# MLP weights of a fused decoder layer: a plain piece as one k tile by 1024 columns instead of two k tiles by 512

## The chip, the core and the metric

The kernel runs as one program on one core of a Trainium2 chip. A core has a matrix engine (TensorE, "PE" in the rows; its weight loads are "PEld"), a vector engine (VectorE, "DVE"), a scalar engine (ScalarE, "ACT"), a general engine (GpSimd, "POOL") and a sync engine (SyncE, "SP"), which here issues every DMA. The engines run their own instruction streams in order and wait for each other by semaphores. The metric is the device time of one execution in microseconds (us), as a median over runs.

## What is computed

One decoder layer in fp32 for 256 tokens and a width of 2048: three token mixers, their gated sum, an output projection, and then the MLP that the change is about.

```python
merged = g[:, :, 0] * o_conv + g[:, :, 1] * o_fox + g[:, :, 2] * o_mem
x = x + merged @ w_out
h2 = _rms(x, norm2_g)
x = x + jnp.square(jax.nn.relu(h2 @ w_up)) @ w_down   # w_up 2048 x 8192, w_down 8192 x 2048
```

## The kernel before

**How products are made.** Tokens are in two tiles of 128 (`TOK = 2`). Activations are the stationary operand (128 by 128), weights the moving one (128 by 512). Each fp32 product is three passes on split operands: low activations by high weights, high by high, high by low. So a weight tile `raw` that DMA brings is split by ScalarE into `whi` (line 591, `split`) and by VectorE into `wlo = raw - whi` (line 1009), and TensorE then uses both. There are `RING = 4` slots of 128 by 1024 for `raw`, `whi` and `wlo`. The semaphore `lo_ready` counts pieces split; `piece_used` counts pieces that TensorE is through with.

**How the MLP is cut.** D_FF is taken in four quarters (`QUARTERS`) of 2048. A quarter has four blocks (`blk` 0 to 3) of 1024 output columns: 0 and 1 multiply by `w_up` (stationary operand `lhs_b`), 2 and 3 by `w_down` (stationary operand `lhs_a`, the squared ReLU of the first two). A block has eight groups of two k tiles (`at` 0 to 7, in the order `K_ORDER`), and a group is 256 rows by 1024 columns of weights. Of the eight groups six are *plain* and two are *fast* (`FAST_AT`): a fast group loads all its 1 MB at once into `raw_f`, and makes seven products in place of eight from sums of weight quarters, formed by VectorE (`t_sums`, lines 1311 to 1316), split by ScalarE (line 794) and VectorE (line 1320); the remaining quarters are split by lines 802 and 1326. Fast products run at line 1801. `raw_f` is a single buffer: SyncE reloads it (line 520) when line 1326 of the fast group before is done. "Fast (3, 5)" below is the one at place 5 of block 3.

A plain group is two *pieces*, n and n + 1, each a 512 KB DMA (line 524) and twelve matmuls (line 1780). Before the change piece n is the *left* half of the block's columns (banks 0 and 1, `side` 0) for both k tiles, and piece n + 1 the *right* half (banks 2 and 3, `side` 1). PSUM banks 0 to 3 hold the block's sums by side and token tile.

**Between blocks.** The sums are copied out of banks 0 and 1, then 2 and 3, by ScalarE (`c_copy`, line 892, 128 by 1024 each, to the buffers named `stage` and `junk`), which counts `c_out`; TensorE may start the next block's left sums after the first copy and its right sums after the second. Blocks 0 to 2 end with a fast group, in which the four banks are finished 15 and 12 matmuls before the group's end. Block 3 ends with a plain group at place 7 (its fast groups are at 2 and 5), and there the first copy waits for the left piece and the second for the right piece. ScalarE's order at the start of a quarter is written out by hand:

```python
upper(0, 0)          # splits of group 0, left and right
if q:
    c_copy(0, 0)
left(0, 1)           # split of the next group's first piece
if q:
    c_copy(0, 1)
right(0, 1)
```

Three places are at such a *quarter boundary*, where a block 3 is followed by a block 0. After the fourth block 3 VectorE adds the result straight from the banks (line 1544 for the left half, two instructions of line 1548 for the right), and SyncE stores the left half in one DMA of 512 KB (line 550) and the right in two of 256 KB (line 555).

Of the kernel before, what the change touches and what calls it, by code (L numbers as in the profile page):

```python
# [25 lines left out]
P = 128  # L26
D = 2048
TOK = 2
KT = D // P
# [7 lines left out]
PK = 2  # L37
# [147 lines left out]
def is_fast(n):  # L185
    if n < first(B_FF):
        return False
    _, blk, at, _ = ff_place(n)
    return at in FAST_AT[blk]
# [73 lines left out]
def build(nc, t, out):  # L263
    ctx = ExitStack()
    with ctx:
# [10 lines left out]
        def sem(name):  # L276
            return ctx.enter_context(nc.semaphore(name))
# [118 lines left out]
        t_made, t_hi_ready, t_lo_ready = sem("t_made"), sem("t_hi_ready"), sem("t_lo_ready")  # L396
        fast_landed, fast_made = sem("fast_landed"), sem("fast_made")
        a_copied, s_made = sem("a_copied"), sem("s_made")
        s_hi_ready, s_lo_ready = sem("s_hi_ready"), sem("s_lo_ready")
# [46 lines left out]
        def _(sp):  # L446
# [66 lines left out]
            def load_ff(n, src, base=0):  # L513

                if is_fast(n):
                    if freed_by(n) < 0:
                        sp.wait_ge(merged_ready, NBD)
                    else:
                        sp.wait_ge(lo_ready, base + (freed_by(n) + 1))
                    sp.dma_start(raw_f[:].rearrange("p (k s) n -> p k (s n)", k=PK), src).then_inc(fast_landed, 16)  # L520
                    return
                sp.wait_ge(lo_ready, base + (freed_by(n) + 1))
                slot = plain(n) % RING
                sp.dma_start(raw[slot], src).then_inc(landed[slot], 16)

            for n in load_order(0):
                _, blk, at, side = ff_place(n)
                k = slice(PK * K_ORDER[blk][at], PK * (K_ORDER[blk][at] + 1))
                c = WIDE * (blk % UPS) + COLS * side
                if is_fast(n) and side:  # L530
                    continue
                width = WIDE if is_fast(n) else COLS
                load_ff(n, w_up[:, k, c:c + width] if blk < UPS else w_down[0, :, k, c:c + width])

            with sp.Fori(0, QUARTERS - 1) as i:
                for n in load_order(1):
                    _, blk, at, side = ff_place(n)
                    k = slice(PK * K_ORDER[blk][at], PK * (K_ORDER[blk][at] + 1))
                    c = WIDE * (blk % UPS) + COLS * side
                    if is_fast(n) and side:  # L540
                        continue
                    width = WIDE if is_fast(n) else COLS
                    if blk < UPS:
                        src = w_up[:, k, bass.ds(i * D + (D + c), width)]
                    else:
                        src = w_down_rows[:, bass.ds(i * KT + (KT + k.start), PK), c:c + width]
                    load_ff(n, src, base=i * FF_PIECES)
# [35 lines left out]
        def _(act):  # L583
# [258 lines left out]
            def quarter(q, i):  # L842
# [39 lines left out]
                def c_copy(blk, side):  # L882

                    pq, pblk, number = block_of_sums(blk)
                    if GROUPS - 1 in FAST_AT[pblk]:
                        act.wait_ge(fast_made, by_f * 5 + (5 * last_fast(pq, pblk) + 1 + side))
                    else:
                        act.wait_ge(piece_used, by_n + (ff_piece(q, blk) - 1 + side))
                    if number:
# [113 lines left out]
        def _(dve):  # L1003
# [538 lines left out]
            dve.wait_ge(x_in, UPS * QUARTERS)  # L1542
            dve.wait_ge(piece_used, ff_piece(QUARTERS) - 1)
            dve.tensor_tensor(x_half(UPS - 1, 0), bank_all[:, 0:2, :], comb[:, 0:2, :],
# [8 lines left out]
        def _(pe):  # L1553
# [217 lines left out]

            def half_group(n, side, k, at, lhs, stops):


                pe.wait_ge(lo_ready, n + 1)
                hi, lo = whi[n % RING], wlo[n % RING]
                for kk in range(PK):
                    for tok in range(TOK):
                        for i, (part, w) in enumerate(((1, hi), (0, hi), (0, lo))):
                            last = pe.matmul(bank[2 * side + tok],  # L1780
                                             lhs[:, part, PK * k + kk, P * tok:P * (tok + 1)], w[:, kk, :],
                                             start=(at + kk == 0 and i == 0),
                                             stop=(tok in stops and kk == PK - 1 and i == 2))
                last.then_inc(piece_used, 1)
# [50 lines left out]
            for n in range(ff_piece(0), ff_piece(QUARTERS)):  # L1835
# [19 lines left out]
                if at == 0 and number == 0:  # L1855
                    pe.wait_ge(dve_emptied, emptied(B_WO + 2))
                elif at == 0:
                    pe.wait_ge(c_out, 2 * (number - 1) + side + 1)
                if number == 0:
# [4 lines left out]
                plain_last = GROUPS - 1 not in FAST_AT[blk]  # L1864
                stops = ()
                if at == GROUPS - 1:
                    stops = (0, 1)
                elif at == GROUPS - 2 and not plain_last and side == 0:
                    stops = (0,)
                half_group(n, side, k, at, lhs, stops)  # L1870

# [36 lines left out]
```

## Time and profile before

| what | us |
|---|---|
| median of 3 runs | 1637.64 (1636.01 to 1638.37) |
| the profiled execution, its own time | 1635.64 |
| its span, first to last instruction | 1633.9 |
| TensorE busy in it | 1624.5 |
| VectorE busy | 1101.9 |
| ScalarE busy | 851.6 |
| granted TensorE clock | 1.000 of full over the span |

The span leaves out 1.74 us of the profiled execution's time. Spans and waits below are from that one execution. A row of the timeline gives start, duration, engine, line, operation, output and inputs, how many instructions were merged in it, and in brackets how long the engine had been idle and whose end released it. Matmuls overlap in the pipeline, so the distance between two starts, not the duration, says how fast they go.

### The profile page before, as it was taken

To read this page: it belongs to the slowest core of one execution; us is meant where nothing else is said; L and a number is where in the kernel's file an instruction comes from. 1 tells how busy PE (TensorE), PEld (TensorE's weight loads), DVE (VectorE), ACT (ScalarE), POOL (GpSimd) and SP (SyncE) were. 2 spreads that over 40 slices of the span, in tenths; PEclk is the share of its full clock that TensorE was granted. 3 is DMA by queue.
4 is the path that set the end of the run, shared out by engine and by line. 5 is a ranking of instruction groups with operands and counts; after the bars stand their busy time and mean duration, and the time that the engine had idled before them with its cause. 6 is when DMAs were issued, how large, how long until landed. Compare 5 with 4: busy or idle time off the path is not lost.

```text
span 1633.9 us, 20167 instructions
## 1 busy us (share of the span) xinstructions
PE 1624.5 (99%) x7404; PEld 1345.7 (82%) x7404; DVE 1101.9 (67%) x1199; ACT 851.6 (52%) x1002; POOL 4.8 (0%) x13
## 2 busy tenths in 40 slices
PE   8999999999999999999999999999999999999998
PEld 7888888888888888888888888888888888888887
DVE  5856666545465444456665678887878788887777
ACT  5844445443454444444344566655665466555663
POOL 0000000000000000000000000000000000000000
PEclk9999999999999999999999999999999999999999
DMA  9866565566666666765666665566656565665554
GB/s 323 286 176 185 166 181 151 158 171 175 170 180 185 194 190 191 199 192 182 197 188 184 209 189 177 192 201 196 204 188 198 191 197 184 203 206 188 191 188 153
DMA packets 151486, 313.70 MB, mean 192 GB/s; under 512 B 9072, under 2 KB 9456, under 8 KB 150896
## 3 DMA queue, kind: packets, MB, share of 16 engines
q1 hardware_dynamic: 151408, 312.62, 62.1%
q8 instruction: 54, 0.88, 0.2%
q14 instruction: 24, 0.20, 0.0%
HBM read 310.49 MB, written 2.10 MB: 191 GB/s over the span
## 4 chain that ended last, share of the span: by engine, by line
PE 93%; DVE 3%; DMA 2%; issue 1%; ACT 1%; SPq 0%; DVEq 0%; ACTq 0%
PE bank L1567 53%; PE bank L1780 28%; PE bank L1801 8%; PE bank L1584 2%; DMA raw_f<-in_w_down 1%; PE bank L1597 1%; DVE wlo L1009 1%; DMA raw<-in_w_mem_kv 1%; DVE wlo L1326 1%; ACT whi L591 0%; DVE t_raw L1311 0%; DVE t_lo L1320 0%; PE bank L1692 0%; PE bank L1622 0%; PE bank L1653 0%
## 5 line engine op out<-in xcount | busy, mean ns | idle before, releaser
L1009 DVE TENSOR_TENSOR wlo<-raw,whi 128x1024 fp32r<-128x1024 f32 x510 | 619.2, 1223 | 440.6 <-ACT whi L591 437.6
L591 ACT ACTIVATE whi<-raw 128x1024 fp32r<-128x1024 f32 x510 | 537.5, 1058 | 585.5 <-PE bank L1567 393.7
L1567 PE MATMUL bank<-whi,lhs_a 128*128 128x512 f32 x1920 | 598.2, 393 | 0.0
L1567 PEld LDWEIGHTS bank<-whi,lhs_a 128*128 128x128 f32 x1920 | 357.2, 188 | 71.7
L1567 PE MATMUL bank<-wlo,lhs_a 128*128 128x512 f32 x960 | 374.7, 390 | 0.0
L1780 PE MATMUL bank<-whi,lhs_b 128*128 128x512 f32 x768 | 237.6, 391 | 0.0
L1780 PE MATMUL bank<-whi,lhs_a 128*128 128x512 f32 x768 | 237.5, 391 | 0.0
L1567 PEld LDWEIGHTS bank<-wlo,lhs_a 128*128 128x128 f32 x960 | 180.3, 188 | 38.1
L1780 PEld LDWEIGHTS bank<-whi,lhs_a 128*128 128x128 f32 x768 | 143.6, 188 | 29.4
L1780 PEld LDWEIGHTS bank<-whi,lhs_b 128*128 128x128 f32 x768 | 143.5, 188 | 29.3
L1567 PE MATMUL bank<-whi,lhs_b 128*128 128x512 f32 x512 | 158.3, 391 | 3.2 <-DVE wlo L1032 2.5
L1780 PE MATMUL bank<-wlo,lhs_b 128*128 128x512 f32 x384 | 149.7, 390 | 0.0
L1780 PE MATMUL bank<-wlo,lhs_a 128*128 128x512 f32 x384 | 149.7, 390 | 0.0
L1567 PEld LDWEIGHTS bank<-whi,lhs_b 128*128 128x128 f32 x512 | 95.7, 188 | 24.1 <-issue 4.5
L1567 PE MATMUL bank<-wlo,lhs_b 128*128 128x512 f32 x256 | 99.8, 390 | 0.0
L1780 PEld LDWEIGHTS bank<-wlo,lhs_a 128*128 128x128 f32 x384 | 72.1, 188 | 15.0
L1780 PEld LDWEIGHTS bank<-wlo,lhs_b 128*128 128x128 f32 x384 | 72.1, 188 | 15.0
L1320 DVE TENSOR_TENSOR t_lo<-t_raw,t_hi 128x2048 fp32r<-128x2048 f32 x32 | 73.1, 2285 | 4.5 <-ACT t_hi L794 4.5
L802 ACT ACTIVATE whi<-raw_f 128x1536 fp32r<-128x1536 f32 x32 | 47.6, 1487 | 54.2 <-PE bank L1780 54.2
L1326 DVE TENSOR_TENSOR wlo<-raw_f,whi 128x1536 fp32r<-128x1536 f32 x32 | 56.1, 1754 | 26.0 <-ACT whi L802 26.0
L794 ACT ACTIVATE t_hi<-t_raw 128x1024 fp32r<-128x1024 f32 x64 | 64.5, 1047 | 13.6 <-DVE t_raw L1311 11.7
L1567 PEld LDWEIGHTS bank<-wlo,lhs_b 128*128 128x128 f32 x256 | 48.0, 188 | 10.1
(200 smaller groups left out, 1253.4 us busy)
## 6 DMA issues: line engine op xcount, KB each, us to landing
raw<-in_w_in SPq DMA_DIRECT2D x208, 512.0 KB, 3.8
raw<-in_w_up SPq DMA_DIRECT2D x96, 512.0 KB, 4.1
raw<-in_w_down SPq DMA_DIRECT2D x96, 512.0 KB, 4.6
raw<-in_w_out SPq DMA_DIRECT2D x32, 512.0 KB, 4.5
raw_f<-in_w_up SPq DMA_DIRECT2D x16, 1024.0 KB, 5.0
raw_f<-in_w_down SPq DMA_DIRECT2D x16, 1024.0 KB, 5.2
raw<-in_w_mem_kv SPq DMA_DIRECT2D x30, 512.0 KB, 6.9
raw<-in_w_conv_out SPq DMA_DIRECT2D x16, 512.0 KB, 4.5
```

Of the source, the lines that this page charges most:

```text
L591: act.activation(whi[n % RING], raw[slot], ACT.Copy).then_inc(hi_ready, 1)
L794: act.activation(t_hi[:, 2 * h:2 * h + 2, :], t_raw[:, 2 * h:2 * h + 2, :], ACT.Copy).then_inc(t_hi_ready, 1)
L802: act.activation(whi_all[:, r:r + 2, :].rearrange("p r n -> p (r n)")[:, COLS:], raw_f[:, 1:4, :].rearrange("p k n -> p (k n)"), ACT.Copy) ...
L1009: dve.tensor_tensor(wlo[n % RING], raw[plain(n) % RING], whi[n % RING].bitcast(F32), ALU.subtract).then_inc(lo_ready, 1)
L1320: dve.tensor_tensor(t_lo[:], t_raw[:], t_hi[:].bitcast(F32), ALU.subtract).then_inc(t_lo_ready, 1)
L1326: dve.tensor_tensor(lo, raw_f[:, 1:4, :].rearrange("p k n -> p (k n)"), hi.bitcast(F32), ALU.subtract).then_inc(lo_ready, 2)
L1567: last = pe.matmul(dst, lhs[:, part, k + kk, s], w[:, kk, :], start=(k + kk == 0 and i == 0), stop=(k + kk == tiles - 1 and i == 2))
L1584: last = pe.transpose(bank[tr_bank(g) if bk is None else bk][:, P * i:P * (i + 1)], src, ident[:])
L1597: last = pe.matmul(dst, a, b, start=(i == 0), stop=(i == len(pairs) - 1))
L1780: last = pe.matmul(bank[2 * side + tok], lhs[:, part, PK * k + kk, P * tok:P * (tok + 1)], w[:, kk, :], start=(at + kk == 0 and i == 0), s ...
L1801: ins = pe.matmul(bank[to], a[part], b[w_part], start=(own and begins and i == 0), stop=(closes and i == 2))
```

## The change

A plain piece keeps its bytes and its twelve matmuls, but is cut the other way: piece n is the group's first k tile by all 1024 columns, piece n + 1 its second k tile. DMA brings rows of 4 KB instead of two rows of 2 KB for each partition. In each piece TensorE makes the left sums with its first six matmuls and the right sums with the last six (`k_tile` in place of `half_group`). The wait for `c_out` of the right side, once at the head of piece n + 1, now stands in the middle of piece n. At the end of block 3 the left sums are finished in the middle of the last piece; a new semaphore `left_made` says so, and the first copy (or line 1544 at the very end) waits for it.

```diff
@@ -395,6 +395,7 @@
         relu_ready, sq_ready = sem("relu_ready"), sem("sq_ready")
         t_made, t_hi_ready, t_lo_ready = sem("t_made"), sem("t_hi_ready"), sem("t_lo_ready")
         fast_landed, fast_made = sem("fast_landed"), sem("fast_made")
+        left_made = sem("left_made")
         a_copied, s_made = sem("a_copied"), sem("s_made")
         s_hi_ready, s_lo_ready = sem("s_hi_ready"), sem("s_lo_ready")
         c_out, p1_copied, combined = sem("c_out"), sem("p1_copied"), sem("combined")
@@ -521,29 +522,31 @@
                     return
                 sp.wait_ge(lo_ready, base + (freed_by(n) + 1))
                 slot = plain(n) % RING
-                sp.dma_start(raw[slot], src).then_inc(landed[slot], 16)
+                sp.dma_start(raw_all[:, slot:slot + 1, :], src).then_inc(landed[slot], 16)
 
             for n in load_order(0):
                 _, blk, at, side = ff_place(n)
                 k = slice(PK * K_ORDER[blk][at], PK * (K_ORDER[blk][at] + 1))
-                c = WIDE * (blk % UPS) + COLS * side
+                c = WIDE * (blk % UPS)
                 if is_fast(n) and side:
                     continue
-                width = WIDE if is_fast(n) else COLS
-                load_ff(n, w_up[:, k, c:c + width] if blk < UPS else w_down[0, :, k, c:c + width])
+                if not is_fast(n):
+                    k = slice(k.start + side, k.start + side + 1)
+                load_ff(n, w_up[:, k, c:c + WIDE] if blk < UPS else w_down[0, :, k, c:c + WIDE])
 
             with sp.Fori(0, QUARTERS - 1) as i:
                 for n in load_order(1):
                     _, blk, at, side = ff_place(n)
                     k = slice(PK * K_ORDER[blk][at], PK * (K_ORDER[blk][at] + 1))
-                    c = WIDE * (blk % UPS) + COLS * side
+                    c = WIDE * (blk % UPS)
                     if is_fast(n) and side:
                         continue
-                    width = WIDE if is_fast(n) else COLS
+                    if not is_fast(n):
+                        k = slice(k.start + side, k.start + side + 1)
                     if blk < UPS:
-                        src = w_up[:, k, bass.ds(i * D + (D + c), width)]
+                        src = w_up[:, k, bass.ds(i * D + (D + c), WIDE)]
                     else:
-                        src = w_down_rows[:, bass.ds(i * KT + (KT + k.start), PK), c:c + width]
+                        src = w_down_rows[:, bass.ds(i * KT + (KT + k.start), k.stop - k.start), c:c + WIDE]
                     load_ff(n, src, base=i * FF_PIECES)
             for c in range(NBD - 1):
                 sp.wait_ge(ff_done, 2 * FF_BLOCKS * (QUARTERS - 1) + 2 * UPS + c + 1)
@@ -884,8 +887,10 @@
                     pq, pblk, number = block_of_sums(blk)
                     if GROUPS - 1 in FAST_AT[pblk]:
                         act.wait_ge(fast_made, by_f * 5 + (5 * last_fast(pq, pblk) + 1 + side))
+                    elif side == 0:
+                        act.wait_ge(left_made, i + (pq + 1))
                     else:
-                        act.wait_ge(piece_used, by_n + (ff_piece(q, blk) - 1 + side))
+                        act.wait_ge(piece_used, by_n + ff_piece(q, blk))
                     if number:
                         act.wait_ge(ff_done, by_8 + 2 * number)
                     act.wait_ge(tr_made, by_8 + (G_FF + GROUPS * pq + 4 * min(pblk, UPS)))
@@ -1540,7 +1545,7 @@
                         ff_piece(QUARTERS - 1, FF_BLOCKS - 1, FAST_AT[-1][-1]) + 1, part)
             x_to_sums(last, UPS - 1)
             dve.wait_ge(x_in, UPS * QUARTERS)
-            dve.wait_ge(piece_used, ff_piece(QUARTERS) - 1)
+            dve.wait_ge(left_made, QUARTERS)
             dve.tensor_tensor(x_half(UPS - 1, 0), bank_all[:, 0:2, :], comb[:, 0:2, :],
                               ALU.add).then_inc(ff_done, 1)
             dve.wait_ge(piece_used, ff_piece(QUARTERS))
@@ -1769,18 +1774,23 @@
                     pe.wait_ge(tr_taken, G_MERGED + m - first(b) + 1)
                 products(m, b, PK * (m - first(b)), lhs_a, KT)
 
-            def half_group(n, side, k, at, lhs, stops):
+            def k_tile(n, number, k, at, lhs, ends_left, ends_all):
 
 
                 pe.wait_ge(lo_ready, n + 1)
-                hi, lo = whi[n % RING], wlo[n % RING]
-                for kk in range(PK):
+                hi, lo = [w[:, n % RING, :].rearrange("p (s n) -> p s n", s=2) for w in (whi_all, wlo_all)]
+                first_of_block, closing = at == 0 and n % 2 == 0, n % 2 == 1
+                for side in range(2):
+                    if first_of_block and number:
+                        pe.wait_ge(c_out, 2 * (number - 1) + side + 1)
                     for tok in range(TOK):
+                        ends = closing and (ends_all or ends_left and side == tok == 0)
                         for i, (part, w) in enumerate(((1, hi), (0, hi), (0, lo))):
                             last = pe.matmul(bank[2 * side + tok],
-                                             lhs[:, part, PK * k + kk, P * tok:P * (tok + 1)], w[:, kk, :],
-                                             start=(at + kk == 0 and i == 0),
-                                             stop=(tok in stops and kk == PK - 1 and i == 2))
+                                             lhs[:, part, k, P * tok:P * (tok + 1)], w[:, side, :],
+                                             start=(first_of_block and i == 0), stop=(ends and i == 2))
+                    if side == 0 and closing and ends_all:
+                        last.then_inc(left_made, 1)
                 last.then_inc(piece_used, 1)
 
             def fast_group(n, q, blk, at, lhs, sums):
@@ -1854,20 +1864,14 @@
                     act_transposes(q, blk, turns[blk, at, side])
                 if at == 0 and number == 0:
                     pe.wait_ge(dve_emptied, emptied(B_WO + 2))
-                elif at == 0:
-                    pe.wait_ge(c_out, 2 * (number - 1) + side + 1)
                 if number == 0:
                     wo_events(n)
                     pe.wait_ge(tr_taken, G_X2 + k + 1)
                 if blk == UPS:
                     pe.wait_ge(tr_taken, G_FF + GROUPS * q + k + 1)
                 plain_last = GROUPS - 1 not in FAST_AT[blk]
-                stops = ()
-                if at == GROUPS - 1:
-                    stops = (0, 1)
-                elif at == GROUPS - 2 and not plain_last and side == 0:
-                    stops = (0,)
-                half_group(n, side, k, at, lhs, stops)
+                k_tile(n, number, PK * k + side, at, lhs, at == GROUPS - 2 and not plain_last,
+                       at == GROUPS - 1)
 
 
 _INS = ["x", "mem", "x_t", "mem_t", "cols", "w_in", "w_mem_kv", "w_conv_out", "w_fox_out",
```

TensorE's order at a quarter boundary, where the last piece of block 3 (operand `lhs_a`) is followed by the first two pieces of block 0 (`lhs_b`); a row may stand for several equal instructions. Before:

```order
L1780 MATMUL bank<-wlo,lhs_a 128x512
L1780 MATMUL bank<-whi,lhs_b 128x512 [waits lo_ready,c_out]
L1780 MATMUL bank<-whi,lhs_b 128x512
L1780 MATMUL bank<-wlo,lhs_b 128x512
L1780 MATMUL bank<-whi,lhs_b 128x512 x2
L1780 MATMUL bank<-wlo,lhs_b 128x512
L1780 MATMUL bank<-whi,lhs_b 128x512 x2
L1780 MATMUL bank<-wlo,lhs_b 128x512
L1780 MATMUL bank<-whi,lhs_b 128x512 x2
L1780 MATMUL bank<-wlo,lhs_b 128x512
L1780 MATMUL bank<-whi,lhs_b 128x512 [waits lo_ready,c_out]
```

The same place after the change:

```order
L1789 MATMUL bank<-wlo,lhs_a 128x512
L1789 MATMUL bank<-whi,lhs_b 128x512 [waits c_out,lo_ready]
L1789 MATMUL bank<-whi,lhs_b 128x512
L1789 MATMUL bank<-wlo,lhs_b 128x512
L1789 MATMUL bank<-whi,lhs_b 128x512 x2
L1789 MATMUL bank<-wlo,lhs_b 128x512
L1789 MATMUL bank<-whi,lhs_b 128x512 [waits c_out]
L1789 MATMUL bank<-whi,lhs_b 128x512
L1789 MATMUL bank<-wlo,lhs_b 128x512
L1789 MATMUL bank<-whi,lhs_b 128x512 x2
L1789 MATMUL bank<-wlo,lhs_b 128x512
L1789 MATMUL bank<-whi,lhs_b 128x512 [waits lo_ready]
```

The second wait for `c_out` has moved from twelve matmuls behind the first to six.

ScalarE's order at the same place, before (`junk<-bank` is the copy of the right sums; ISA and REGISTER_ALU rows are waits and the arithmetic of their values):

```order
L591 ACTIVATE whi<-raw 128x1024 [waits piece_used]
L888 REGISTER_ALU
L890 ISA [waits piece_used]
L891 REGISTER_ALU [waits ff_done]
L892 ACTIVATE stage<-bank 128x1024 [waits tr_made]
L591 ACTIVATE whi<-raw 128x1024 [waits piece_used,landed2]
L888 REGISTER_ALU
L892 ACTIVATE junk<-bank 128x1024 [waits tr_made,ff_done,piece_used]
L591 ACTIVATE whi<-raw 128x1024 [waits piece_used,landed3]
```

And after:

```order
L594 ACTIVATE whi<-raw 128x1024 [waits piece_used]
L891 REGISTER_ALU
L895 ISA [waits left_made]
L896 REGISTER_ALU [waits ff_done]
L897 ACTIVATE stage<-bank 128x1024 [waits tr_made]
L593 REGISTER_ALU [waits landed2]
L594 ACTIVATE whi<-raw 128x1024 [waits piece_used]
L893 REGISTER_ALU
L897 ACTIVATE junk<-bank 128x1024 [waits tr_made,ff_done,piece_used]
L594 ACTIVATE whi<-raw 128x1024 [waits piece_used,landed3]
```

ScalarE's order is the same, with a split between the two copies; only what releases the first copy has changed.

## Rows read from the trace of the kernel before

**Rows 1.** Page, parts 1 and 3: engines' busy time; DMA queue, packets, MB, share.

```profile
PE 1624.5 (99%) x7404; PEld 1345.7 (82%) x7404; DVE 1101.9 (67%) x1199; ACT 851.6 (52%) x1002; POOL 4.8 (0%) x13
...
q1 hardware_dynamic: 151408, 312.62, 62.1%
```

**Rows 2.** All waits of TensorE from 820 us to the end: total, times, longest.

```profile
PE bank L1801 <- DVE wlo L1326: 0.3, 1, 0.3
```

**Rows 3.** Timeline, TensorE, first quarter boundary (block 3 to block 0).

```profile
1109.27 0.39 PE L1780 MATMUL bank<-wlo,lhs_a 128*128 128x512 f32 x1
...
1110.63 0.39 PE L1780 MATMUL bank<-wlo,lhs_a 128*128 128x512 f32 x1
...
1111.99 0.39 PE L1780 MATMUL bank<-wlo,lhs_a 128*128 128x512 f32 x1
1112.22 0.62 PE L1780 MATMUL bank<-whi,lhs_b 128*128 128x512 f32 x2
...
1113.58 0.62 PE L1780 MATMUL bank<-whi,lhs_b 128*128 128x512 f32 x2
```

**Rows 4.** Timeline, ScalarE, the same boundary.

```profile
1109.86 1.03 ACT L892 ACTIVATE stage<-bank 128x1024 f32<-128x1024 f32 x1 [1.82 <-PE bank L1780]
1110.78 1.05 ACT L591 ACTIVATE whi<-raw 128x1024 fp32r<-128x1024 f32 x1
1112.42 1.03 ACT L892 ACTIVATE junk<-bank 128x1024 f32<-128x1024 f32 x1 [0.59 <-PE bank L1780]
```

**Rows 5.** Timeline, ScalarE, the third quarter boundary: first copy.

```profile
1454.49 1.03 ACT L892 ACTIVATE stage<-bank 128x1024 f32<-128x1024 f32 x1 [1.81 <-PE bank L1780]
```

**Rows 6.** Timeline, first block boundary: the right sums' copy, the next block's first matmul.

```profile
978.94 1.02 ACT L892 ACTIVATE junk<-bank 128x1024 f32<-128x1024 f32 x1
...
981.22 0.62 PE L1780 MATMUL bank<-whi,lhs_b 128*128 128x512 f32 x2
```

**Rows 7.** Timeline, VectorE, block 3 of the first quarter.

```profile
1068.96 1.23 DVE L1311 TENSOR_TENSOR t_raw<-raw_f 128x1024 f32<-128x1024 f32 x1 [1.70 <-DMA raw_f<-in_w_down]
...
1095.31 1.75 DVE L1326 TENSOR_TENSOR wlo<-raw_f,whi 128x1536 fp32r<-128x1536 f32 x1
```

**Rows 8.** Timeline, TensorE, fast (3, 5) of the first and last quarter.

```profile
1095.97 0.62 PE L1801 MATMUL bank<-t_hi,lhs_a 128*128 128x512 f32 x2
...
1097.12 0.73 PE L1801 MATMUL bank<-whi,s_down 128*128 128x512 f32 x2 [0.31 <-DVE wlo L1326]
...
1097.92 0.63 PE L1801 MATMUL bank<-whi,lhs_a 128*128 128x512 f32 x2
...
1613.49 0.62 PE L1801 MATMUL bank<-t_hi,lhs_a 128*128 128x512 f32 x2
...
1615.07 0.62 PE L1801 MATMUL bank<-whi,lhs_a 128*128 128x512 f32 x2
```

**Rows 9.** Timeline, the tail: VectorE, SyncE, TensorE.

```profile
1627.31 1.23 DVE L1544 TENSOR_TENSOR x_sb<-bank,comb 128x1024 f32<-128x1024 f32 x1
...
1628.56 0.37 SPq L550 DMA_DIRECT2D out<-x_sb  x1
...
1629.15 0.39 PE L1780 MATMUL bank<-wlo,lhs_a 128*128 128x512 f32 x1
1629.58 1.29 DVE L1548 TENSOR_TENSOR x_sb<-bank,comb 128x512 f32<-128x512 f32 x2 [1.05 <-PE bank L1780]
1630.30 0.94 SPq L555 DMA_DIRECT2D out<-x_sb  x2
```

**Rows 10.** Windows of 1 us: busy time by engine, clock, DMA share, GB/s.

```profile
1060.00:1061.00 1.00, 1.00 (x6) 0.84 (x5) 1.00 (x1) 1.00 (x1) 0.00 (x0) 1.00 0.75 281
...
1067.00:1068.00 1.00, 1.00 (x6) 0.84 (x5) 0.27 (x1) 1.00 (x2) 0.00 (x0) 1.00 1.04 426
...
1629.00:1630.00 1.00, 0.54 (x3) 0.12 (x1) 0.42 (x1) 0.00 (x0) 0.00 (x0) 1.00 0.55 209
...
1632.00:1633.00 1.00, 0.00 (x0) 0.00 (x0) 0.00 (x0) 0.00 (x0) 0.00 (x0) 0.63 0.57 203
```

## The prediction

> **What bounds the kernel now.** The page's first part comes first: TensorE is busy for 1624.5 of 1633.9 us [rows 1], far ahead of the other engines. Next the waits, cut to the stretch from 820 us to the end, which holds the whole MLP (it begins near 940 us): TensorE's only wait on the list is one of 0.3 us [rows 2]. So the engine that the change touches has no idle time to give back there, and anything the change does to DMA, to ScalarE or to VectorE shows in the time only where it makes TensorE wait or spares it this one wait. Third, the timeline of TensorE gives its pace: six matmuls of 512 columns from 1112.22 to 1113.58 us, that is 1.36 us for six, 0.227 us each, 2.72 us for a piece [rows 3]. The clock column stands at 1.00, the higher of the two levels (2.4 GHz), in the windows shown while matmuls run [rows 10].
>
> **The matmuls.** The change makes the same twelve matmuls for each of the 192 plain pieces, with the same operand sizes, each preceded by the same weight load, and still three in a row on one bank before the next. I cost this at nothing: 0. It is the only edit with a large multiplier (2304 matmuls), and nothing in it that a row could price has changed.
>
> **The DMAs.** Bytes and the number of transfers stay. A 512 KB transfer falls from 256 rows of 2 KB to 128 of 4 KB, so of the 151,408 packets [rows 1] 192 x 128 = 24,576 go. No transfer of a plain piece holds TensorE [rows 2], so the cover is TensorE itself; without it, a landing late by d costs d. One chain does touch a landing, that of `raw_f` for block 3. In the first quarter VectorE waits 1.70 us for it until 1068.96 us, then works without a longer gap than the wait for line 794 up to the end of line 1326 at 1095.31 + 1.75 = 1097.06 us [rows 7], and TensorE's second product of fast (3, 5) starts at 1097.12, 0.06 us later [rows 8]. From the first product's start to the third's start should be six matmuls, 1.36 us; it is 1097.92 - 1095.97 = 1.95 us, a loss of 0.59, and in the last quarter 1615.07 - 1613.49 = 1.58 us, a loss of 0.22 [rows 8]. The list of waits counts only 0.3 of the 0.59 as waited. The two middle quarters lie between nothing and the last one's 0.22; I take 0.05 each. Together some 0.9 us could be won if `raw_f` landed earlier, and 4 us are lost for each microsecond that it lands later, once in each quarter. How does a landing move? A window with plain transfers only moved 281 GB/s at a share of 0.75, that is 375 at full share; one with `raw_f` rows of 4 KB in it 426 at 1.04, that is 410 [rows 10]. Rows of 4 KB are at best 9% quicker, and `raw_f` itself keeps its shape; only the plain transfers around it gain, about 0.1 us on one of 512 KB (0.52 MB at some 400 GB/s are 1.3 us of flow). I take 0.2 us as won in all, with 0 to 0.9 as the bounds on the winning side.
>
> The Trainium skill, "Perfetto Trace Analysis", section "DMA Optimizations", says that batching 2 KB transfers into 4 or 8 KB can dramatically improve throughput where the kernel is DMA-bound. The rows above show 9% at best, and no DMA that TensorE waits for directly. By that rule the winning bound of 0.9 us would be reached, and the sum below would be 1.7 in place of 2.4 us.
>
> **The quarter boundaries (three of them).** Here a cover goes. Before, the left sums were done at the left piece's last matmul, which starts at 1109.27; the first copy starts at 1109.86, 0.59 later [rows 3, 4], while the right piece still runs for 2.72 us. The third boundary has the same form: a copy of 1.03 us after 1.81 us of idleness [rows 5]. The right copy starts at 1112.42, which is 0.43 after the last matmul's start at 1111.99, and is over at 1113.45 [rows 3, 4]; right matmuls came only at 1112.22 + 2.72 = 1114.94. Now:
>
> 1. The last left matmul of block 3 starts at 1110.63 [rows 3], where the first half of the last piece ends. With the same 0.59, the first copy starts at 1111.22 and ends at 1112.25.
> 2. TensorE wants to start block 0 at 1112.22 [rows 3]. With 0.06 us from the end of the releasing instruction it starts at 1112.31: late by 0.09. A restart costs more than the wait: three matmuls from the one released at 1097.12 take until 1097.92, 0.80 us, where three take 0.68 at the pace, that is 0.12 more [rows 8]. So 0.21.
> 3. ScalarE has a split between the copies. One instruction follows another by 0.92 us (1110.78 - 1109.86) [rows 4]. The split starts at 1112.14 and, itself some 0.95 long in pace, lets the second copy start at 1113.09, over at 1114.11.
> 4. TensorE wants the right banks 1.36 us after its start, which was at 1113.58 before [rows 3]. It gets them at 1114.11 + 0.06 = 1114.17, and with the 0.12 of a restart it stands 1114.17 - 1113.58 + 0.12 = 0.71 us behind. This contains the 0.21 of step 2, since the second copy doesn't wait for TensorE's restart.
>
> So 0.71 us for each boundary, three times: **2.1 us**. What is queued behind: ScalarE's next split starts at 1114.02 in place of 1113.34, 0.7 later, and all of its later work is for pieces that TensorE reaches more than 5 us on; VectorE has its own work until then. I see no second stall behind the first. Bounds: 0 if the copies hide (a rival), 3 x (0.71 + 0.43) = 3.4 if the second copy also showed the 0.43 us of release that it has behind an idle ScalarE.
>
> **The other block boundaries (twelve).** The fast group at the end finishes the banks early: the right copy runs from 978.94 to 979.96 and the next block starts at 981.22 [rows 6]. The right half now wants it at 982.58 in place of 983.94; more than 2.6 us are left. 0.
>
> **The tail.** Line 1544 started at 1627.31, held by VectorE's work before it and not by TensorE. The last matmul starts at 1629.15 [rows 9], so the last left one, six earlier, at 1627.79; with the 0.43 that line 1548 shows from the last matmul to its start (1629.58) line 1544 now starts at 1628.22, 0.91 later, and is over at 1629.45, just before line 1548 can begin. The store of the left half is issued 0.91 later too, at 1629.47, and the two stores of the right at 1630.30 as before [rows 9]. All 1 MB of output then flows closer together: the flow began in the window 1629 to 1630, with a share of 0.55, and ended in that of 1632 to 1633, with 0.57 [rows 10], and had slack of a few tenths between. I take **0.5 us**, with bounds of 0 (the later stores hide it) and 0.9 (the whole shift).
>
> **Sum.** 2.1 + 0.5 - 0.2 = +2.4 us on the profiled execution's 1635.64 us, of which 1633.9 are span. That execution lies 2.0 us below the median of the runs, 1637.64, with nothing to say that the change would treat them differently, so I add to the median: **1640.0 us**, +0.15%. A measurement of this kernel tells about 0.2% (3.3 us) from no change, so I forecast a small loss that counts as the same.
>
> **The rivals.**
> - *The landing of `raw_f` comes later and decides (slower).* Place: block 3 of each quarter, before line 1311. Its chain has no slack in any quarter [rows 7, 8], so d later costs 4d. With +2.6 from boundaries and tail, d = 0.2 us is enough to pass 3.3 us; with d = 0.5 the time is 1637.64 + 2.6 + 2.0 = 1642.2. For it: transfers share the 16 engines, and a plain transfer between two of `raw_f`'s packets now comes in packets of twice the bytes. Against it: `raw_f` is issued ahead of those, and its own rows are of 4 KB already beside them. 0.18.
> - *The copies hide after all.* If the first copy is released 0.2 us sooner than I take (0.43, as line 1548 and the right copy show, in place of 0.59), 0.16 of each boundary goes; if `raw_f` gains its 0.9 as well, the sum is 3 x 0.55 + 0.3 - 0.9 = +1.0; with no stall at all at the boundaries, +0.3 - 0.9 = -0.6. Times 1637.0 to 1638.7. 0.15.
> - *DMA was holding more than the waits show, and 4 KB rows free it.* All that TensorE loses in the MLP to other engines is the 0.9 us above; even if all of it is won and nothing lost the time is 1636.7, so faster by 0.2% (below 1634.4) needs matmuls themselves to go faster. 0.04.
>
> **How the numbers follow.** The forecast has 0.63, with a range of its own from 1639.0 (a boundary at 0.5, tail 0.1, `raw_f` -0.2) to 1641.0 (boundaries at 0.9, tail 0.9, no gain). Slower by over 0.2% is above 1640.9: the first rival and a sliver of the forecast, 0.20. Faster 0.04. The same 0.76. The range reaches from 1637.4 to 1642.0.
>
> **What would show it.** In the changed kernel's waits TensorE should have a wait for ScalarE's copy line three times, 0.3 to 0.6 us each, and the distance from the first to the seventh matmul of block 0 at a boundary should be near 1.36 + 0.5 us. The first copy should start about 1.2 us nearer to the new block. The pace elsewhere stays 0.227 us. In the tail line 1544's successor starts about 0.9 us later and the store's end moves by half of that. DMA packets fall by 24,576. If TensorE shows no such wait, step 3 (the split between the copies) is wrong; if the pace of matmuls differs, the zero for the matmuls is; if VectorE's wait for `raw_f` in block 3 changes by more than 0.2 us, the first or third rival holds.

## The result: +0.16%, a small loss that counts as the same

| | kernel before | changed kernel |
|---|---|---|
| median of 22 runs each, us | 1636.04 (1634.49 to 1638.89) | 1638.61 (1637.28 to 1641.13) |
| ratio, 95% interval | | 1.0016 (1.0009 to 1.0022) |
| span of the profiled execution, us | 1633.9 | 1636.1 |

The change costs 2.6 us by the medians and 2.2 us between the two profiled spans. +2.4 us was forecast. The interval of the ratio lies above 1, so the loss is real, though far below what counts as slower. Runs of one kernel spread over some 4 us, which is more than the effect; the last section shows where a part of that may come from. So the medians decide little between versions that differ by 1 us, and the readings below rest mainly on the traces.

The forecast time, 1640.0 us, lies 1.4 us above the measured 1638.61. Most of that is the base and not the change forecast upon it: the three runs known beforehand had a median of 1637.64 us, the 22 runs here have 1636.04.

The page of the changed kernel, the lines that answer to [rows 1], and the median landing of its transfers:

```profile
PE 1625.8 (99%) x7404; PEld 1344.5 (82%) x7404; DVE 1102.2 (67%) x1199; ACT 851.9 (52%) x1002; POOL 4.8 (0%) x13
...
q1 hardware_dynamic: 126832, 312.62, 61.2%
...
raw<-in_w_up SPq DMA_DIRECT2D x96, 512.0 KB, 4.4
raw<-in_w_down SPq DMA_DIRECT2D x96, 512.0 KB, 4.5
raw_f<-in_w_up SPq DMA_DIRECT2D x16, 1024.0 KB, 5.1
```

TensorE has the same 7404 matmuls. The queue's packets fell by 151,408 - 126,832 = 24,576, and its share from 62.1 to 61.2%: the wider rows are there, and they save 1.5% of the DMA engines' time. In the kernel before the same three medians were 4.1, 4.6 and 5.0 us: landings are not sooner by more than 0.1 us, and the first are later.

The only wait of the changed kernel's matmuls from 820 us on, and the two longest of its weight loads; the first list had one row for VectorE before [rows 2]:

```profile
PE bank L1789 <- ACT junk L897: 0.2, 1, 0.2
...
PEld bank L1789 <- ACT junk L897: 1.7, 3, 0.6
PEld bank L1789 <- issue: 1.2, 3, 0.4
```

The weight loads of the kernel before, all waits from 820 us on:

```profile
PEld bank L1801 <- DVE wlo L1326: 1.5, 4, 0.7
PEld bank L1584 <- ACT stage L905: 0.5, 1, 0.5
```

A wait that is new, for ScalarE's copy of the right sums (line 897 is 892 of the kernel before), three times, up to 0.6 us. The three of 0.4 us, for which the profile names no releaser, stand ahead of the first matmul of the block 0 at each boundary, where the first copy is waited for. Most of the waiting is put down to the weight loads, so the list of TensorE's matmul waits alone shows only 0.2 us. The distance of starts in the timeline has no such blind spot. Here is TensorE at the first quarter boundary, to be held against [rows 3]:

```profile
1111.53 0.39 PE L1789 MATMUL bank<-wlo,lhs_a 128*128 128x512 f32 x1
1111.93 0.70 PE L1789 MATMUL bank<-whi,lhs_b 128*128 128x512 f32 x2
1112.46 0.40 PE L1789 MATMUL bank<-wlo,lhs_b 128*128 128x512 f32 x1
...
1113.69 0.73 PE L1789 MATMUL bank<-whi,lhs_b 128*128 128x512 f32 x2
1114.26 0.40 PE L1789 MATMUL bank<-wlo,lhs_b 128*128 128x512 f32 x1
1114.49 0.62 PE L1789 MATMUL bank<-whi,lhs_b 128*128 128x512 f32 x2
```

And ScalarE there, to be held against [rows 4]:

```profile
1110.75 1.03 ACT L897 ACTIVATE stage<-bank 128x1024 f32<-128x1024 f32 x1 [3.17 <-PE bank L1789]
1111.68 1.05 ACT L594 ACTIVATE whi<-raw 128x1024 fp32r<-128x1024 f32 x1
1112.62 1.02 ACT L897 ACTIVATE junk<-bank 128x1024 f32<-128x1024 f32 x1
```

At the pace of 0.227 us block 0 would begin at 1111.53 + 0.23 = 1111.76; its first matmul starts at 1111.93, late by 0.17 (0.15 behind the end of the first copy, 1110.75 + 1.03 = 1111.78), and the next start loses another 0.08. The right half wants to start 1.36 us on, at 1113.12 by the unhindered count, and does at 1113.69; after the restart the third-next start is 1114.49 where 1113.80 was due, so the boundary costs 0.69 us (0.71 by the thirteenth matmul, the measure of the table below). ScalarE sat idle 3.17 us before the first copy, then did copy, split, copy without a gap, and the second copy's end, 1112.62 + 1.02 = 1113.64, is followed 0.05 us later by the held matmul. The other two boundaries agree with this one within 0.02 us.

The tail of the changed kernel, timeline rows of the engines that [rows 9] show for the kernel before:

```profile
1629.87 1.23 DVE L1549 TENSOR_TENSOR x_sb<-bank,comb 128x1024 f32<-128x1024 f32 x1 [1.02 <-PE bank L1789]
...
1630.73 0.39 PE L1789 MATMUL bank<-wlo,lhs_a 128*128 128x512 f32 x1
1631.12 0.37 SPq L553 DMA_DIRECT2D out<-x_sb  x1
1631.16 1.29 DVE L1553 TENSOR_TENSOR x_sb<-bank,comb 128x512 f32<-128x512 f32 x2
1631.88 1.01 SPq L558 DMA_DIRECT2D out<-x_sb  x2
```

The left half's addition started 1.84 us before the last matmul, and now starts 0.86 before; now TensorE holds it, not VectorE. The right half's stores are issued 1.15 us behind the last matmul in both. From the last matmul's start to the span's end it was 1633.9 - 1629.15 = 4.75 us and is 1636.1 - 1630.73 = 5.37: 0.6 us more.

Between the first matmul of the MLP (938.10 before, 938.21 after) and the last, TensorE took 691.05 us before and 692.52 after. This *MLP stretch* (+1.47) and the tail (+0.6) are the measures used below.

### The profile page after: what moved, and what is told of

Its sections match the earlier page's. It is cut to its first block, busy times and chain, and to the rows that moved or that the text cites. A ratio compares the mean times of both kernels' runs of the same rounds, so it can differ in the third digit from the quotient of the medians.

```text
span 1636.1 us, 20156 instructions
## 1 busy us (share of the span) xinstructions
PE 1625.8 (99%) x7404; PEld 1344.5 (82%) x7404; DVE 1102.2 (67%) x1199; ACT 851.9 (52%) x1002; POOL 4.8 (0%) x13
## 3 DMA queue, kind: packets, MB, share of 16 engines
q1 hardware_dynamic: 126832, 312.62, 61.2%
## 4 chain that ended last, share of the span: by engine, by line
PE 98%; DMA 1%; ACT 0%; DVE 0%; issue 0%; SPq 0%; ACTq 0%; DVEq 0%
PE bank L1572 53%; PE bank L1789 32%; PE bank L1811 9%; PE bank L1589 2%; PE bank L1602 1%; DMA raw<-in_w_mem_kv 1%; PE bank L1697 0%; ACT whi L594 0%; PE bank L1627 0%; PE bank L1658 0%; DVE wlo L1014 0%; PE bank L1717 0%; ACT junk L897 0%; PE bank L1622 0%; PE bank L1719 0%
```

## The experiments

All are timed beside the kernel before on the same chip; the ratio is to it. The table has what the traces gave; the MLP stretch runs from the start of the first MLP matmul to the start of the last, the tail from there to the span's end. "Boundaries" is how far the thirteenth matmul of a block 0 starts behind the pace, counted from the last matmul of the block 3 before it, summed over the three places. "Fast (3, 5)" is what its third product starts later than 1.36 us behind its first, summed over the four quarters.

| kernel | MLP stretch | boundaries | fast (3, 5) | tail | median, us | ratio (95% interval) |
|---|---|---|---|---|---|---|
| before | 691.05 | 0.00 | 0.90 | 4.75 | 1636.04 | |
| changed | 692.52 | 2.13 | 0.37 | 5.37 | 1638.61 | 1.0016 (1.0009 to 1.0022) |
| 1. both copies first | 691.32 | 0.87 | 0.61 | 5.4 | 1638.37 | 1.0013 (1.0004 to 1.0022) |
| 2. both splits between the copies | 695.10 | 4.96 | 0.22 | 5.4 | 1641.23 | 1.0036 (1.0022 to 1.0050) |
| 3. last group as before | 690.40 | 0.17 | 0.28 | 4.75 | 1636.73 | 1.0007 (0.9998 to 1.0016) |
| 4. before, last group alone changed | 691.21 | 0.63 | 0.55 | 5.5 | 1637.06 | 1.0006 (0.9997 to 1.0015) |
| 5. load of `raw_f` later | 711.24 | 2.15 | 1.11 | 5.4 | 1655.37 | 1.0119 (1.0104 to 1.0134) |
| 6. last group as before, sums early | 689.97 | 0.18 | 0.00 | 4.8 | 1635.06 | 0.9998 (0.9989 to 1.0007) |
| 7. before, sums early | 689.78 | 0.00 | 0.00 | 4.8 | 1634.95 | 0.9996 (0.9987 to 1.0005) |

The median of the kernel before lay between 1635.6 and 1636.2 us beside the experiments.

**1. Both copies first.** Is it the split between the two copies that makes the second one late?

```diff
                 if q:
                     c_copy(0, 0)
-                left(0, 1)
-                if q:
                     c_copy(0, 1)
-                right(0, 1)
+                upper(0, 1)
```

> The changed kernel with ScalarE's order at a quarter boundary altered: both copies of the sums first, then the two splits of group 1. My theory (the second copy is late by the split that stands between the copies): the second copy starts when the last piece is used, so TensorE's right half no longer waits; of the 0.70 us lost at each boundary 0.5 goes and the wait for the first copy, 0.18, stays. So 1.5 us below the changed kernel, about +1.1 us on the kernel before (+0.07%). Rival (the loss is the late release of the first copy, or the middle-of-piece wait itself): nothing gained, +2.6 us.

The gaps of 0.31 us ahead of the right half are gone at all three boundaries; what stays is 0.17 us ahead of block 0, 0.08 at the next start and 0.04 around the middle of the piece. So a boundary still costs 0.29 us and not the 0.2 that was expected to stay. The MLP stretch fell from 692.52 to 691.32, by 1.2 us, where 1.5 were expected. The tail is that of the changed kernel, as it should be, so by the trace it stands 0.3 + 0.65 = 0.9 us above the kernel before. The ratio's interval holds this and holds the changed kernel's loss too: the medians don't tell the two apart, the trace does. The rival falls.

**2. Both splits between the copies.** The same cost, doubled.

```diff
                 if q:
                     c_copy(0, 0)
-                left(0, 1)
+                upper(0, 1)
                 if q:
                     c_copy(0, 1)
-                right(0, 1)
```

> The changed kernel with the suspected cost doubled: both splits of group 1 stand between the two copies. My theory: the second copy starts one more split (0.93 us) later, so each boundary loses 0.70 + 0.93 = 1.6 us, three boundaries 4.9; the whole is 2.8 us above the changed kernel, about +5.4 us on the kernel before (+0.33%). Rival (the order on ScalarE is not what holds TensorE): no change, +2.6 us.

Timeline of TensorE at its first boundary, where the right half starts:

```profile
1113.84 0.73 PE L1788 MATMUL bank<-whi,lhs_b 128*128 128x512 f32 x2 [1.09 <-ACT junk L897]
```

The gap ahead of the right half rose from 0.31 to 1.26 us, by 0.95, which is one split in pace. The boundaries together rose from 2.13 to 4.96 us, the 2.8 that was expected; the MLP stretch rose by 695.10 - 692.52 = 2.6 us, since fast (3, 5) lost 0.15 less in this execution. The ratio is 1.0036, where +5.4 us is 1.0033. ScalarE's order at this place is priced: 0.94 us for each split that stands ahead of the second copy.

**3. The last group of block 3 as before, all other plain pieces changed.** Is there a cost outside the boundaries and the tail, in the shape itself?

```diff
+OLD_CUT = (FF_BLOCKS - 1, GROUPS - 1)
...
-                    elif side == 0:
-                        act.wait_ge(left_made, i + (pq + 1))
                     else:
-                        act.wait_ge(piece_used, by_n + ff_piece(q, blk))
+                        act.wait_ge(piece_used, by_n + (ff_piece(q, blk) - 1 + side))
...
+                if (blk, at) == OLD_CUT:
+                    half_group(n, side, k, lhs)
+                    continue
```

> The changed kernel, but the last plain group of block 3 is loaded and multiplied as before the change (two k tiles by 512 columns, left piece then right piece); the other 44 of 48 plain pieces of each quarter are one k tile by 1024. My theory: the left sums are done a whole piece before the end again, so the first copy, its split and the second copy are in time, and line 1544's work and its store too. The 2.1 us of the boundaries and the 0.6 us of the tail go, and the 0.5 us that fast (3, 5) won stays: 0.5 us below the kernel before, within what a measurement tells (-0.03%), and 2.7 us below the changed one. Rival (the mid-piece wait at the start of a block costs by itself, or the piece's shape does): it stays 1 to 2 us above the kernel before.

(The last group is two pieces, so 46 of the 48 have the new cut, not 44.) Of 0.71 us at a boundary 0.06 is left, the MLP stretch is 690.40, 0.65 below the kernel before, and the tail is back at 4.75 us. The 0.06 is the wait for the second copy, which here too stands in the middle of block 0's first piece. The copy ends 0.13 us before the right half is due, so its matmul is not late; but the weight load ahead of that matmul comes earlier and is held. The row of experiment 6, which has the same boundary (line 908 is the copy):

```profile
1112.25 0.30 PEld L1801 LDWEIGHTS bank<-whi,lhs_b 128*128 128x128 f32 x2 [0.18 <-ACT junk L908]
```

The matmuls behind the held weight load lose those 0.06 us, and this is the only place where experiments 6 and 7 differ in pace. The median doesn't show the gain (ratio 1.0007, interval from 0.9998). The profiled execution says why a single one misleads: its span is 1635.0, 1.1 above the kernel before, with a faster MLP; its MLP begins 1.75 us late, at 939.85, for a reason that lies in the first 20 us (last section).

**4. The kernel before with the last group alone changed.** The complement.

```diff
+NEW_CUT = (FF_BLOCKS - 1, GROUPS - 1)
...
+                    elif side == 0:
+                        act.wait_ge(left_made, i + (pq + 1))
                     else:
-                        act.wait_ge(piece_used, by_n + (ff_piece(q, blk) - 1 + side))
+                        act.wait_ge(piece_used, by_n + ff_piece(q, blk))
...
+                if (blk, at) == NEW_CUT:
+                    k_tile(n, PK * k + side, lhs)
+                    continue
```

> The kernel before with one part of the change alone: only the last group of block 3 is cut as one k tile by 1024 columns. My theory: the first copy is released 1.36 us later and TensorE waits for it at the boundary (0.2 us, three times), but the right half is wanted only 2.72 us on, after the second copy, so the other 0.5 us is not lost; the tail loses its 0.6 us. Together +1.2 us on the kernel before (+0.07%). Rival (the late end of the left sums alone makes the whole loss): +2.7 us.

The MLP stretch is 691.21 and the tail 5.5: +0.2 and +0.7, together 0.9 us where 1.2 was expected and the rival had 2.7. A boundary loses 0.21 us, 0.08 ahead of block 0 and the rest right behind it, 0.6 for the three as expected; fast (3, 5) lost 0.35 less than in the kernel before. So 0.2 of a boundary's 0.7 us comes with the left sums that end late, and the other 0.5 needs both halves of the change: these, and the right half that is wanted early. The tail's loss needs the first alone.

**5. The load of `raw_f` for fast (3, 2) issued behind the next plain load.** This prices the rival that would have made the kernel slower.

```diff
-    return sorted(range(ff_piece(q), ff_piece(q + 1)), key=lambda n: (freed_by(n), n))
+    order = sorted(range(ff_piece(q), ff_piece(q + 1)), key=lambda n: (freed_by(n), n))
+    n = ff_piece(q, 3, 2)
+    at = order.index(n)
+    order.remove(n)
+    plains = [i for i, m in enumerate(order) if i >= at and not is_fast(m)]
+    order.insert(plains[0] + 1, n)
+    return order
```

> The changed kernel, with SyncE issuing the 1 MB load for fast (3, 2) behind the plain load that used to follow it, once in each quarter, so about 1.1 us or more later. It prices the rival that a later landing would have decided. The chain from this landing through VectorE to fast (3, 5) has 0.02 to 0.14 us of loss in the changed kernel's quarters, so no slack: my theory says TensorE loses 1.0 to 1.5 us more at fast (3, 5) or (3, 2) in each of four quarters, 4 to 6 us on the changed kernel, +7 to +8 us on the kernel before (+0.45%). Rival (VectorE's gaps further on take the delay up): less than 1 us on the changed kernel, +2.6 to +3.5 us on the kernel before.

+19.8 us on the kernel before by the medians, far more than the +7 to +8 of my theory. Timeline of SyncE, VectorE and TensorE in its first quarter:

```profile
1064.52 0.44 SPq L527 DMA_DIRECT2D raw_f<-in_w_down  x1
...
1071.37 1.23 DVE L1322 TENSOR_TENSOR t_raw<-raw_f 128x1024 f32<-128x1024 f32 x1 [4.53 <-DMA raw_f<-in_w_down]
...
1076.63 0.74 PE L1795 MATMUL bank<-whi,lhs_a 128*128 128x512 f32 x2 [2.00 <-DVE wlo L1020]
```

Three things were mis-sized. The load was issued 1.2 us later than in the changed kernel (1063.34), as thought, but it also took 6.85 us to land in place of 5.16. It now stands behind 512 KB issued just before it, which I take for the reason; that was not tested apart. VectorE's first sum comes at 1071.37 in place of 1068.50, 2.9 us late and not 1.2. Second, the first to suffer is not a fast group but a plain piece: the split of group (3, 1) is queued behind the sums on VectorE, and TensorE waits 2.2 us for it, then 0.9 more at fast (3, 5). Third, in the three later quarters the load took still longer (7.28, 7.06 and 7.76 us), the wait is longer, and TensorE's granted clock falls behind it. Windows around the wait of the second, and behind that of the last quarter (the last three figures are granted clock, DMA share and GB/s):

```profile
1254.00:1257.00 3.00, 2.96 (x7) 2.38 (x8) 3.00 (x3) 0.00 (x0) 0.00 (x0) 0.50 0.54 161
1257.00:1259.00 2.00, 2.00 (x9) 1.63 (x9) 2.00 (x2) 0.36 (x1) 0.00 (x0) 0.90 0.68 231
...
1613.00:1616.00 3.00, 3.00 (x8) 2.31 (x8) 3.00 (x3) 0.85 (x1) 0.00 (x0) 0.53 0.48 173
```

0.50 is the lower level, 1.2 GHz, behind gaps of 3.2 and 3.4 us ahead of a matmul. It was read behind the third quarter's gap of 2.7 us too (0.53 from 1431.4 to 1435 us); behind the first quarter's gap of 2.2 us it stayed at 1.00. The price of this landing is then about 1.1 us per microsecond in the first quarter (3.2 for 2.9), and more in the quarters where the clock fell. So the rival's price of a microsecond for each microsecond held where the clock stayed up, the place where it shows was wrong, and it did not happen: the landing did not move (below).

**6. and 7. The sums of fast (3, 5) one split earlier on VectorE**, once on the kernel of experiment 3, once on the kernel before.

```diff
-                lower(3, 4)
+                left(3, 4)
                 t_of(3, 5)
+                right(3, 4)
```

> The kernel with the last plain group of block 3 cut as before and all other plain pieces one k tile by 1024, and one move on VectorE besides: the sums of fast (3, 5), lines 1311 to 1316 of the kernel before, ahead of the split of the second piece of group (3, 4) instead of behind it. My theory: nothing is left at the boundaries and the tail, and fast (3, 5) is ready 1 us earlier, so the MLP stretch is 690.3 us against 691.05 of the kernel before, the tail 4.75 us as before: 0.8 us below the kernel before (-0.05%), too little for the measurement to tell, to be read in the trace. Rival (the cut costs something that the boundaries don't show): above the kernel before.

> The kernel before with only that move on VectorE (sums of fast (3, 5) one split earlier). It tests that VectorE's chain, not the shape of the weight rows, is what makes fast (3, 5) late. My theory: the 0.9 us that the four quarters lose there falls to under 0.1 us, with rows of 2 KB as before: the MLP stretch is 690.2 us against 691.05, -0.9 us (-0.05%). Rival (the loss comes from DMA and its row size): the losses at fast (3, 5) stay between 0.05 and 0.6 us a quarter and the time stays.

In the kernel before with this move alone, VectorE's last step for fast (3, 5), and TensorE there, to be held against [rows 7, 8]:

```profile
1093.88 1.75 DVE L1326 TENSOR_TENSOR wlo<-raw_f,whi 128x1536 fp32r<-128x1536 f32 x1
...
1095.91 0.62 PE L1802 MATMUL bank<-t_hi,lhs_a 128*128 128x512 f32 x2
...
1097.27 0.62 PE L1802 MATMUL bank<-whi,lhs_a 128*128 128x512 f32 x2
```

From the first product's start to the third's it is 1.36 us, the bare pace; it was 1.95. VectorE is done at 1095.63, 1.4 us sooner: 1.1 of it because it no longer stands idle for ScalarE between the sums and line 1320, 0.3 because `raw_f` landed sooner in this execution. In all four quarters the third product of fast (3, 5) is on time. The stretch is 689.78, 1.27 below the kernel before, where 0.9 was expected: 0.90 at fast (3, 5), 0.21 because a wait for ScalarE at 1036 us (the weight load of line 1584 above) is gone, the rest in steps too small to name. On the kernel of experiment 3 it is 689.97, and the 0.2 us between the two are the 0.06 at each boundary. So the new cut of 46 pieces in 48 and the old one have the same pace everywhere else, and the lateness of fast (3, 5) was VectorE's order. Both medians lie below the kernel before (by 0.5 and 0.7 us), within the interval; a version that is measurably faster was not found.

## Why the prediction was right

**The matmuls, cost 0: right.** The pace was 0.227 us in every kernel, and experiments 6 and 7 put the two cuts 0.2 us apart over 690 us, all of it at the three boundaries.

**The quarter boundaries, +2.1 us: right in form and size.** 0.71 us for each was forecast, 0.71 was measured. Each link that sets the sum held: first copy released by the last left matmul (0.59 us behind that matmul's start was forecast; the matmul starts at 1110.17, the copy at 1110.75, so 0.58), split in between, second copy's end, held matmul 0.05 us later, restart 0.12 us. Step 2, which the second copy covers, was off in its parts: the first held matmul follows the first copy by 0.15 us and not 0.06, and its restart costs 0.08 and not 0.12. Experiment 1 took away the second link, experiment 2 doubled it, experiment 3 took away the first, and experiment 4 left the first alone: the gaps moved as the chain says. What the chain lacks is the 0.06 us of the wait in the middle of a piece, which showed only where nothing larger stood there.

**The tail, +0.5 us: right, 0.6 measured.** The three stores now flow in one piece. Windows of the changed kernel (DMA's share is the last figure but one) against the shares of 0.55 and 0.57 at the two ends before [rows 10]:

```profile
1631.00:1632.00 1.00, 0.12 (x1) 0.00 (x0) 0.94 (x3) 0.00 (x0) 0.00 (x0) 1.00 0.00 0
1632.00:1633.00 1.00, 0.00 (x0) 0.00 (x0) 0.44 (x1) 0.00 (x0) 0.00 (x0) 1.00 0.98 373
1633.00:1634.00 1.00, 0.00 (x0) 0.00 (x0) 0.00 (x0) 0.00 (x0) 0.00 (x0) 1.00 1.02 387
1634.00:1635.00 1.00, 0.00 (x0) 0.00 (x0) 0.00 (x0) 0.00 (x0) 0.00 (x0) 1.00 0.82 289
```

**`raw_f`, -0.2 us: the term's mechanism was wrong, its size by luck not far off.** I had the gain come from quicker plain rows. In the profiled execution fast (3, 5) did lose less: in the first quarter it took 1097.45 - 1095.95 = 1.50 us from first to third product in place of 1.95, and over all four quarters the loss fell from 0.90 to 0.37, so the gain was 0.5 us. But the wider rows did not do it. From issue to the start of VectorE's first sum, over all fast groups where it waited for the landing, I read a mean of 5.32 us before and 5.24 and 5.21 in experiments 4 and 7 (the kernel before with the sums early), which have rows of 2 KB throughout or nearly so, against 5.24 in the changed kernel and 5.30, 5.14, 5.21 and 5.22 in experiments 1, 2, 3 and 6, with rows of 4 KB: no difference beyond the scatter. What differed in the first quarter was one landing earlier in the chain, that of fast (2, 7). It scatters by itself, and with VectorE's order unchanged the loss of fast (3, 5) in the first quarter goes with it: 6.69 us and a loss of 0.59 before, 6.38 and 0.23 in experiment 1, 6.21 and 0.14 changed, and 0.02 in experiments 3, 4 and 2, where it took 6.10, 5.82 (with rows of 2 KB) and 5.12 us. So the kernel before happened to be profiled with a late landing, and nothing shows that the 0.5 us are the change's. The Trainium skill ("Perfetto Trace Analysis", "DMA Optimizations") states its rule on larger transfers for a DMA-bound kernel. Here the queue's share fell from 62.1 to 61.2% and no median landing came sooner by more than 0.1 us.

**The time itself: inside the range, from a base that was off.** The stretch and the tail together rose by 1.47 + 0.6 = 2.1 us, where 2.4 was forecast. But 1638.61 us lies below the forecast's own range of 1639.0 to 1641.0 and inside the 1637.0 to 1638.7 of the second rival, whose mechanism (copies that hide) is refuted by the three waits. (By the terms it names, that range would end at 1641.2.) The median of three runs was 1.6 us above that of 22, and the +2.4 us were added to it. The waits of the weight loads were not listed either: the 0.9 us taken as all that TensorE loses to other engines left out the 0.21 at 1036 us.

**The other block boundaries, 0: right.** The changed kernel has no gap over 0.1 us at any of them, and experiments 6 and 7 have the same pace across all twelve.

## What to carry to other kernels

When one engine is busy 99% of the time, a change of tiling that leaves its work alone has little to win (here TensorE's waits were worth 1.3 us of 691), and what it loses, it loses at the joints. Look for the places where a result is finished in one piece and its room wanted in the next, and write down both times before and after. Here the left sums ended half a piece later and the right room was wanted half a piece earlier, and a hand-written order on another engine, harmless before, stood between them. A cost of 2 us in 1640 is below what a few runs tell, but starts of matmuls in the trace show it: the three boundaries agreed within 0.02 us. Compare a stretch and a tail, not whole spans.

## What the runs showed of the hardware that was not expected

**The first 20 us differ between executions, and move the span by 1.75 us.** The first MLP matmul came near 938.0 us (937.70 to 938.34) in seven of the profiled executions above, but at 939.88 and 939.85 in those of experiments 1 and 3. Windows of 3 us in the kernel before, and in experiment 3:

```profile
14.00:17.00 3.00, 2.37 (x11) 1.65 (x10) 1.91 (x4) 1.54 (x3) 0.00 (x0) 1.00 0.97 353
17.00:20.00 3.00, 2.89 (x13) 2.11 (x12) 2.39 (x4) 2.54 (x5) 0.00 (x0) 1.00 1.03 406
```

```profile
14.00:17.00 3.00, 1.37 (x5) 1.20 (x6) 2.02 (x3) 2.09 (x4) 0.00 (x0) 0.93 0.99 358
17.00:20.00 3.00, 3.00 (x8) 2.34 (x7) 2.38 (x4) 2.31 (x5) 0.00 (x0) 0.50 1.04 408
```

In the first TensorE works for 2.37 of 3 us and keeps the full clock; in the second it works for 1.37, waiting for the first weights, and then runs at 0.50, the lower level, so that 17 to 20 us hold 8 matmuls instead of 13. The two kernels differ there in nothing but line numbers, and the 1.75 us that experiment 3 is behind at 20 us are still 1.75 at the first MLP matmul. Such a start in some executions would be one reason why medians of 5 to 11 runs stray by up to a microsecond; the other runs have no trace to show it.

**A stall costs more than its wait.** Behind each held matmul the next starts come 0.08 to 0.13 us later than the pace, wherever the clock stayed up. And of the 2.1 us that the boundaries cost, the list of TensorE's matmul waits showed 0.2.

**A held weight load costs time though no matmul is late for its own wait.** In experiment 6 the matmul of the right half started on time; but the weight load ahead of it had waited 0.18 us, and the next few starts lost 0.06 us between them, at each of the three boundaries.
